# Products of a constant in TensorE's norm waits, and an earlier start for the squares of a post norm

## The reference

```
for i in range(2):
    h = rms_norm(x, norm_w[i, 0]) * (1 + sc_m) + sh_m          # pre norm
    y = mixer(h)                                               # in-projections, heads, out-projection (16 units)
    x = x + g_m * rms_norm(y, norm_w[i, 1])                    # post norm
    h = rms_norm(x, norm_w[i, 2]) * (1 + sc_f) + sh_f          # pre norm
    y = (gelu(conv(h @ w_up)[gate]) * conv(h @ w_up)[val]) @ w_down   # ConvFFN: 44 up units, 22 down units
    x = x + g_f * rms_norm(y, norm_w[i, 3])                    # post norm
```

## Time and profile before

| | us |
|---|---|
| median of 3 runs (1235.38 to 1236.77) | 1235.38 |
| the profiled execution | 1234.31 |
| its span on the engines | 1232.5 |
| PE busy | 1125.3 (91%) |
| DVE busy | 883.5 (72%) |
| ACT busy | 628.2 (51%) |
| mean granted clock of TensorE | 0.953 |

### The profile page before, as it was taken

The page is one execution under the profiler, slowest core; times in us unless marked ns, Lnnn a source line. Parts: engine busy times, 40 slices in busy tenths (PEclk is TensorE's granted clock), DMA queues, the critical chain, the costliest instruction groups (busy, mean ns, idle before and its releaser), DMA issues.

```text
span 1232.5 us, 28100 instructions
## 1 busy us (share of the span) xinstructions
PE 1125.3 (91%) x10161; PEld 1088.7 (88%) x10161; DVE 883.5 (72%) x1909; ACT 628.2 (51%) x1317; POOL 21.0 (2%) x12
## 2 busy tenths in 40 slices
PE   5899999989899999989999997589986989999996
PEld 5899988979899999989999985579876989999996
DVE  3587646669778889976888674876644886888854
ACT  1376455344366665445666536166524445666542
POOL 0000000000000000000000001200100000000000
PEclk9899899999889999987999998789999998999998
DMA  9457534627636566932766521013202662666661
GB/s 358 151 172 238 177 122 141 197 84 292 254 104 186 178 181 221 342 118 78 228 223 187 188 70 35 2 40 88 83 1 92 208 249 75 184 185 179 180 200 56
DMA packets 54830, 195.58 MB, mean 159 GB/s; under 512 B 6067, under 2 KB 8115, under 8 KB 54492
## 3 DMA queue, kind: packets, MB, share of 16 engines
q1 hardware_dynamic: 54748, 194.45, 48.2%
HBM read 193.36 MB, written 1.07 MB: 158 GB/s over the span
## 4 chain that ended last, share of the span: by engine, by line
PE 68%; DVE 6%; ACT 2%; issue 1%; DVEq 0%; ACTq 0%
PE proj L507 43%; PE acc L507 25%; DVE off_bd L1677 1%; DVE state L1751 1%; PE acc L688 0%; DVE sys_t L1685 0%; DVE yr L1492 0%; DVE o_tok L1778 0%; DVE yr L1469 0%; DVE k_tok L1667 0%; DVE conv L1698 0%; DVE w_lo L1345 0%; ACT w_hi L1003 0%; DVE dec L1660 0%; DVE ada_sum L1359 0%
## 5 line engine op out<-in xcount | busy, mean ns | idle before, releaser
L1003 ACT ACTIVATE w_hi<-raw 128x512 fp32r<-128x512 f32 x528 | 328.7, 625 | 178.6 <-PE acc L507 127.9
L1345 DVE TENSOR_TENSOR w_lo<-raw,w_hi 128x512 fp32r<-128x512 f32 x528 | 358.8, 684 | 79.0 <-ACT w_hi L1003 77.8
L507 PE MATMUL proj<-h_hi,w_hi 128*128 128x256 f32 x1352 | 389.8, 288 | 4.0 <-DVE h_lo L1465 3.7
L507 PE MATMUL proj<-h_lo,w_hi 128*128 128x256 f32 x1352 | 386.1, 286 | 0.0
L507 PE MATMUL proj<-h_hi,w_lo 128*128 128x256 f32 x1352 | 385.9, 285 | 0.0
L507 PEld LDWEIGHTS proj<-h_hi,w_hi 128*128 128x128 f32 x1352 | 262.9, 194 | 6.7 <-issue 4.0
L507 PEld LDWEIGHTS proj<-h_lo,w_hi 128*128 128x128 f32 x1352 | 263.5, 195 | 0.0
L507 PEld LDWEIGHTS proj<-h_hi,w_lo 128*128 128x128 f32 x1352 | 263.1, 195 | 0.0
L507 PE MATMUL acc<-a_hi,w_hi 128*128 128x256 f32 (+1 forms) x608 | 172.5, 284 | 3.6 <-DVE a_lo L1632 2.0
L507 PE MATMUL acc<-a_lo,w_hi 128*128 128x256 f32 (+1 forms) x608 | 170.4, 280 | 0.0
L507 PE MATMUL acc<-a_hi,w_lo 128*128 128x256 f32 (+1 forms) x608 | 170.3, 280 | 0.0
(11 more groups left out here) (259 smaller groups left out, 1564.3 us busy)
## 6 DMA issues: line engine op xcount, KB each, us to landing
raw<-in_w_stream SPq DMA_DIRECT2D x264, 512.0 KB, 3.6
ada_long<-in_ada_stream SPq DMA_DIRECT2D x52, 512.0 KB, 6.9
ada_first<-in_ada_stream SPq DMA_DIRECT2D x20, 512.0 KB, 4.4
ada_ssd<-in_ada_stream SPq DMA_DIRECT2D x12, 512.0 KB, 4.5
ada_out<-in_ada_stream SPq DMA_DIRECT2D x12, 512.0 KB, 4.8
hankel<-bias_scratch SPq DMA_DIRECT2D x2, 1024.0 KB, 6.1
x<-in_x_tiles SPq DMA_DIRECT2D x1, 1024.0 KB, 10.5
out_tiles<-x SPq DMA_DIRECT2D x1, 1024.0 KB, 3.9
```

Of the source, the lines that this page charges most:

```text
L507: return pe.matmul(out, a, b, start=start, stop=stop, skip_group_check=True)
L1003: act.activation(hi, src, ACT.Copy).then_inc(w_rounded, 1)
L1345: dve.tensor_tensor(lo, src, hi.bitcast(F32), ALU.subtract).then_inc(w_split, 1)
```

## The change

Two things. TensorE gets a function `keep_busy`, called after `root_mean_square` of events 1 to 6: two fp32 products of the identity with the first columns of `cst`, 512 wide after post norms and 256 wide after pre norms, into the bank of the next unit, whose first product overwrites it. Nothing reads them and they count no semaphore. And ScalarE's squares of a post norm wait for `w_used` per bank instead of once: those of AB[0] and AB[1] for the first half of the last unit, those of AB[2] and AB[3] for its end.

```diff
+            def keep_busy(event, count, width):
+
+                n = PARTS[("dt0", "up0", "up0", "dt1", "dt1", "up1", "up1")[event]][0]
+                s, at, _ = freed[before[n]] if before[n] is not None else (prm_ready, 1, 1)
+                pe.wait_ge(s, at)
+                for _ in range(count):
+                    mm(PB[FIRST_AFTER[event]][:, 0:width], C("ident"), cst[:, 0:width])
...
             root_mean_square(1)
+            keep_busy(1, 2, 512)
             root_mean_square(2)
+            keep_busy(2, 2, 256)
             project("up0", norm=1)
...
             root_mean_square(3)
+            keep_busy(3, 2, 512)
             root_mean_square(4)
+            keep_busy(4, 2, 256)
             project("dt1", token=True, norm=2)
...
             root_mean_square(5)
+            keep_busy(5, 2, 512)
             root_mean_square(6)
+            keep_busy(6, 2, 256)
             project("up1", norm=3)
...
             def post_norm(event, name):
-                act.wait_ge(w_used, 2 * (PARTS[name][0] + PARTS[name][1]))
                 for q in range(4):
+                    act.wait_ge(w_used, 2 * (PARTS[name][0] + PARTS[name][1]) - (1 if q < 2 else 0))
                     act.activation(sq[:, 2 * q:2 * q + 2].rearrange("p a t -> p (a t)"), AB[q][:, :], ACT.Square).then_inc(squares, 2)
```

## The result

The changed kernel takes 1222.5 us (median of 4 runs, 1219.9 to 1224.31) against 1235.41 before: 12.9 us less, a ratio of 0.9883 with a 95% interval of 0.986 to 0.9906. The forecast was 1229.4 with a range from 1223.5: the direction was right, the gain was twice the 6.0 us forecast. The profiled execution took 1221.61 us (span 1219.8) with a mean granted clock of 0.969 instead of 0.953.

What follows compares the result with a forecast made beforehand. The prediction took TensorE, 68% of the span, as the bound, through its pace and its waits. Gains 5.8 + 1.0 - 1.2 + 0.4 = 6.0 us from 1234.31 gave 1228.3, plus 1.1 for the median 1229.4; range 1223.5 to 1235.2.

Steps and rivals of the forecast that it cites:

- the first mechanism: Waits after post norms: the 512-wide products keep TensorE's clock up through the pre norm sums; 5.8 us gained.
- What is late next: First units behind the pre norms: the clock still falls, a little later, and comes back later; 1.2 us lost.
- `dt1` at 1.0: Unit dt1 after event 4: 256-wide products hold the clock longer into it; 1.0 us gained, bounds 0 and 4.4.
- the late low clock at -1.2: Behind the three first units: low stretch ends later; 1.2 us lost together, bounds -2 (a gain) and +10.
- The 512-wide products hidden, at no cost: Events 1, 3, 5: products lie in the wait for squares, 0.9 us to spare; cost 0, without cover 2.4.
- The sums at 5.8 of 6.7 us gained: Pre norm sums of events 2, 4, 6: 6.7 us if the clock holds all through, 5.8 taken.
- The earlier squares at 0.4: Event 7 only: first two squares start half a unit earlier, sums follow earlier; 0.4 us gained, bounds 0 and 0.45.
- Rival C: First units up0, dt1, up1: the clock holds through them too, 7.8 us more gained, 1220.5 us; chance 0.14.
- Rival B: Units TensorE bounds: low clock not avoided but moved onto them, 3.1 us slower, 1238.5 us; chance 0.07.
- Rival A: Waits after the norms: the clock falls all the same, only event 7 gains 0.4 us, 1235.0 us; chance 0.12.

Runs made afterwards that it cites:

- squares_only: The kernel before with only the per-bank waits for the squares and no added products; 1235.0 us, ratio 0.9992.
- narrow_only: The changed kernel without the 512-wide products after post norms (events 1, 3, 5); 1228.6 us, ratio 0.9943 to the kernel before.
- wide_only: The changed kernel without the 256-wide products after pre norms (events 2, 4, 6); 1230.1 us, ratio 0.9948 to the kernel before.
- half_dose: The changed kernel with one added product instead of two in each place; 1230.1 us, ratio 0.995 to the kernel before.
- fill_more: event0_too with constants also multiplied in four further waits (v0, value transposes, inversion, output transposes); 1217.4 us, ratio 0.9851 to the kernel before.
- event0_too: The changed kernel with two 256-wide products after event 0 as well; 1218.0 us, ratio 0.9886 to the kernel before.
- fuller: fill_more with three products instead of two in each of the seven norm waits; 1214.3 us, ratio 0.9828 to the kernel before.

## Why the prediction was wrong

Its direction and the first mechanism were right; its size failed at one step, in "What is late next": "The clock will still fall in the first unit, a little later than before, and then also come back later". It did not fall in the changed kernel, in neither of its two profiles. Two terms of the sum rest on that step, `dt1` at 1.0 and the late low clock at -1.2, and both were wrong. Point by point:

- The 512-wide products hidden, at no cost: right. Four records at 0.43 us, ended 0.98 us before the sums. The sums at 5.8 of 6.7 us gained: 6.07 measured to the first product of the units (2.09 + 2.07 + 1.91). Right in this pair of profiles; as the shorter sums in `squares_only` and `narrow_only` show, the price of an unfilled wait varies by over 1 us from place to place.
- `dt1` at 1.0, between 0 and 4.4: it gained 4.37, the upper bound. Wrong by 3.4.
- The low clock that comes back late, a loss of 1.2: instead the stretches behind the three first units are gone, which gave 0.98 + 1.08 + 1.04 = 3.1. Wrong by 4.3, and beyond the bound of -2 that I gave for no low stretch at all.
- The earlier squares at 0.4: 0.46 measured, in event 7 alone, and nothing in events 1, 3 and 5, for the reason given (the last rounding stands between). Right.
- Not in the sum at all: the part before event 1, where no instruction changed, took 1.4 us longer in this execution, about what `dt0` lost to its longer low stretch. Over the profiles of this study that part, from event 0's sums to event 1's, varies by 4 us with the same code, 285.9 to 289.9, with the low stretches in `dt0` and `v0` beginning elsewhere. The kernel before itself has single times from 1231.6 to 1241.7. The three runs shown at first, within 1.4 us, hid that.

Rival C had the mechanism, and its price for the units was good: 7.8 us, against 4.37 + 3.1 = 7.5 measured. I gave it 0.14. What I held against it was `dt0`, "in which the clock fell in the middle of the unit without any pause of that kind". But there was nearly such a pause: TensorE waits 1.84 us right ahead of it, as it says in the row itself. `dt0` was a case of an unfilled wait like those that the change fills, so it said nothing on what a filled one does; with the wait filled, `dt0` held in two profiles of four. The other error was to reason that a unit in which TensorE waits for tiles of h would mostly bring the clock down by itself. `narrow_only` shows that it need not: behind 0.9 us of products the clock stays at 1.00 through a unit with that same rhythm, and `wide_only` that without them it falls in the first microsecond. Something of the argument stands: in 4 of 27 such units the clock fell in spite of the filled wait.

Rival B, the low clock moved on to dense work, is what half a dose does in part: in `half_dose` the clock fell 3 us into `dt1`. But there was still a gain of 6 us. Rival A was wrong from the sums on.

What is left open: why one execution holds the clock in `dt0` or `up1` and another with the same instructions around it doesn't. The traces show where the step comes (48.7 in `fill_more`, none in `event0_too`), not what decides; whether more products in the wait make it rarer, the six executions of `fuller` don't settle, and its profile still has a fall in `up1`.

## What to carry to other kernels

When a granted clock falls at a wait, count its price to the point where it is back, and not to the end of the operation behind the wait: here half of it or more lay in the units behind the norms (7.5 us in the table, against 6.1 in the sums). A short wait is worth filling with products nobody reads, if a free bank is at hand and they end before the wait does; half the filling gave half the gain, and a filled wait made the falls rare, not impossible. Before a row of the trace is used as a counter-example, look at what stood right ahead of it: the idle time in brackets is part of the row.

## What was not expected of the hardware

- Transposes hold the clock too: 14 of them, 1.69 us, with 1.17 us of idle time behind, and the sums at 1.00 in all three places; 1221.2 us for the whole kernel.
- The same TensorE instructions at the same distances gave 5.91 us and 8.51 us for `dt0` in two executions, of `event0_too` and `fill_more`, at clocks of 1.00 and of 0.50 from 48.7 us on. A single profile of a kernel with such waits is good to some 4 us, and three runs that agree within 1.4 us may still be a narrow sample of a spread of 10.
